# A head's tail interleaved with the next head's first projection, the halves of its output normed apart, and 12 products ahead of the decay gates

## The reference

```
proj = einsum('btd,dn->btn', xn, w_in)          # 1024 -> q, k, v, z_gla, a_lo, gate_logits, ...
g = log_sigmoid(a_lo @ w_a2 + b_a) / GATE_NORM  # decay gates, per head 128 keys
b = cumsum(g) in a chunk
o = (q k^T * decay) v + (q * exp(b)) S          # S: state, 128 x 256 per head
S_new = exp(b_last) * S + (k * exp(b_last - b))^T v
o = o * rsqrt(mean(o * o) + EPS) * gla_norm_g   # per head, over its 256 value channels
y_b = (o * silu(z_gla)) @ w_gla_o
```

## Time and profile before

| | |
|---|---|
| median of 3 runs | 1179.35 us (1177.84 to 1181.88) |
| the profiled execution: device time | 1183.72 us |
| the profiled execution: span | 1182.0 us, mean granted TensorE clock 0.986 |
| PE busy | 1148.5 us (97%) |
| DVE, ACT, POOL busy | 542.8, 425.2, 199.9 us |
| one head on PE, from one diagonal step to the next | 106.8 to 108.3 us |

### The profile page before, as it was taken

One profiled execution on the slowest core, in us unless ns is written; L12 is line 12 of the kernel. 1 busy time (PEld: TensorE's weight loads), 2 busy tenths in 40 slices (PEclk: granted clock), 3 DMA queues, 4 the chain that ended last, 5 costly groups with the idle time before them and its releaser, 6 DMA issues.

```text
span 1182.0 us, 17776 instructions
## 1 busy us (share of the span) xinstructions
PE 1148.5 (97%) x6872; PEld 1108.8 (94%) x6872; DVE 542.8 (46%) x716; ACT 425.2 (36%) x561; POOL 199.9 (17%) x128
## 2 busy tenths in 40 slices
PE   5899999999999999999999999999999999999997
PEld 5899999999999999999999999999999999999886
DVE  5777777775000001663494358437635001444433
ACT  5555555554111112542543453345426111211321
POOL 3511111111212120211112011111101211210000
PEclk8999999999999999999999899999989999999999
DMA  6211111111211222210311131021102103342231
GB/s 211 65 40 47 50 40 40 40 36 37 83 63 54 72 73 62 72 37 18 113 35 35 36 95 35 18 87 48 31 18 76 49 22 110 109 161 83 98 106 71
DMA packets 95631, 76.16 MB, mean 64 GB/s; under 512 B 3944, under 2 KB 88808, under 8 KB 95608
## 3 DMA queue, kind: packets, MB, share of 16 engines
q1 hardware_dynamic: 84588, 61.59, 17.5%
q10 hardware_dynamic: 11020, 14.26, 3.6%
HBM read 62.04 MB, written 13.80 MB: 64 GB/s over the span
## 4 chain that ended last, share of the span: by engine, by line
PE 87%; issue 6%; DVE 4%; ACT 2%; DMA 0%; DVEq 0%; ACTq 0%
PE ps L464 25%; PE ps L465 25%; PE ps L466 25%; PE ps L599 2%; PE ps L662 1%; PE ps L641 1%; PE ps L633 1%; PE ps L643 1%; PE ps L626 1%; DVE xcs L1232 1%; PE ps L681 1%; ACT xcs L891 1%; PE ps L570 1%; DVE xc L1224 1%; PE ps L491 1%
## 5 line engine op out<-in xcount | busy, mean ns | idle before, releaser
L464 PE MATMUL ps<-xn,whi 128*128 128x364 f32 x1344 | 452.2, 336 | 2.4 <-DVE xn L1159 1.5
L465 PE MATMUL ps<-xn,whi 128*128 128x364 f32 x1344 | 443.5, 330 | 0.0
L466 PE MATMUL ps<-xn,wlo 128*128 128x364 f32 x1344 | 443.1, 330 | 0.0
L432 POOL TENSOR_TENSOR wlo<-raw,whi 128x1024 fp32r<-128x1024 f32 x72 | 181.3, 2518 | 862.8 <-ACT whi L838 862.8
L464 PEld LDWEIGHTS ps<-xn,whi 128*128 128x128 f32 x1344 | 254.1, 189 | 6.8 <-issue 2.2
L465 PEld LDWEIGHTS ps<-xn,whi 128*128 128x128 f32 x1344 | 254.3, 189 | 0.2
L466 PEld LDWEIGHTS ps<-xn,wlo 128*128 128x128 f32 x1344 | 254.0, 189 | 0.0
L838 ACT ACTIVATE whi<-raw 128x1024 fp32r<-128x1024 f32 x72 | 76.0, 1055 | 152.1 <-PE ps L466 86.4
L465 PE MATMUL ps<-act_s,whi 128*128 128x364 f32 x384 | 126.2, 329 | 0.0
L464 PE MATMUL ps<-act_s,whi 128*128 128x364 f32 x384 | 126.2, 329 | 0.0
L466 PE MATMUL ps<-act_s,wlo 128*128 128x364 f32 x384 | 126.1, 328 | 0.0
(11 more groups left out here) (246 smaller groups left out, 1389.5 us busy)
## 6 DMA issues: line engine op xcount, KB each, us to landing
raw<-in_w_in SPq DMA_DIRECT2D x56, 512.0 KB, 3.8
branch_a<-keep ACTq DMA_DIRECT2D x8, 546.0 KB, 2.8
mal<-branch_a SPq DMA_DIRECT2D x8, 544.0 KB, 4.5
xt<-in_x_prompt SPq DMA_DIRECT2D x8, 512.0 KB, 6.8
raw<-in_w_lru_o SPq DMA_DIRECT2D x8, 512.0 KB, 3.7
st<-in_state_gla ACTq DMA_DIRECT2D x4, 1024.0 KB, 5.6
out<-st ACTq DMA_DIRECT2D x4, 1024.0 KB, 4.7
raw<-in_w_gla_o SPq DMA_DIRECT2D x8, 512.0 KB, 5.7
```

Of the source, the lines that this page charges most:

```text
L432: pool.tensor_tensor(wlo[:, c % 2], raw[:, c % 2], whi[:, c % 2].bitcast(F32), ALU.subtract).then_inc(s["lo_ok"], 1)
L464: pe.matmul(dst, wh, mh, start=first, stop=False)
L465: pe.matmul(dst, wh, ml, start=False, stop=False)
L466: return pe.matmul(dst, wl, mh, start=False, stop=last)
```

## The change

PE: job 0 of head 0 runs ahead of the loop. In the loop job 5 ends ahead of the outputs, and the tail is interleaved with job 0 of the next head (`part(6, bankA, ...)`; after the last head that is merge-gate job 0): seven groups of three products in Os, then mean squares, then the sample state sums, with products between all. The next head starts with 12 products of job 1, then g0 and g1, 12 more, g2. Steps are renumbered so that nrm0 to nrm2 come ahead of sKV0 to sKV3; g0 and g1 now wait for DVE's sKV2 and sKV3.

ACT: the loads of `wa2_raw` go to SP, the rounding of `wa2` into the tail of the head before. Tanh of job 5 moves ahead of the outputs. Rounding the weights of job 2 moves from ahead of the gates to behind Ln; that of job 3, and the load of the sample states, behind the second level. Ln and Exp write into a half of `qk`, not `kt`. The last head is written out behind a loop of three.

DVE: the two halves are normed and gated apart (`gated_output`): half 0 after sKV1, half 1 after sKV3, each with its own semaphore.

```
@@ sync
                     load(6 * h + (N_GLA + j), (N_GLA + j) % 2, ...)
+                    if j == 0:
+                        sp.wait_ge(s["wa2_lo"], h + ONE)
+                        for r in range(6):
+                            sp.dma_start(wa2_raw[...], t["w_a2"][0][:, bass.ds(h * P, P)]).then_inc(s["wa2_in"], 16)
@@ tensor, Os
-                    between = iter(range(2, KT - 1))
+                    between = iter(range(KT))
-                            if q in (2, 5) or (q == NSEQ - 1 and d == 0):
+                            if q % 2 == 1 and (d == 0 or q < NSEQ - 1):
                                 k = next(between)
-                                part(5, bankB, 2, range(k, k + 1))
+                                part(6, bankA, 0, range(k, k + 1))
@@ tensor, start of a head
-                start_job(0)
+                pe.wait_ge(s["wa2_lo"], h + (ONE + 1))
+                start_job(1)
                 pe.wait_ge(s["zg_silu"], 2 * h + ONE)
-                part(0, bankA, 0)
-                part(0, bankA, 1)
-                part(0, bankA, 2)
+                part(1, bankB, 0, EARLY)
                 gate(0)
                 gate(1)
-                start_job(1)
-                part(1, bankB, 0)
+                part(1, bankB, 0, LATE)
                 gate(2)
@@ tensor, tail
-                part(5, bankB, 2, range(2))
+                part(5, bankB, 2)
...
+                start_job(6)
                 c_step("Os", sample_output)
+                part(6, bankA, 0, range(KT - 1, KT))
+                pe.wait_ge(s["sq_sum"], 2 * h + 1)
+                mean_square(0)
+                part(6, bankA, 1, range(0, 2))
+                mean_square(1)
+                part(6, bankA, 1, range(2, 6))
+                pe.wait_ge(s["sq_sum"], 2 * (h + 1))
+                mean_square(2)
+                part(6, bankA, 1, range(6, KT))
                 sample_outer(0)
+                part(6, bankA, 2, range(0, 1))
                 sample_outer(1)
-                part(5, bankB, 2, range(KT - 1, KT))
+                part(6, bankA, 2, range(1, 3))
                 sample_outer(2)
+                part(6, bankA, 2, range(3, 5))
                 sample_outer(3)
-                for j in range(PIECES):
-                    mean_square(j)
+                part(6, bankA, 2, range(5, KT))
 
-            with pe.Fori(0, KT // 2) as i:
+            job(0, N_GB + 1, bankB, xn)
+            with pe.Fori(1, KT // 2) as i:
@@ scalar
-                hi(3 * h, N_GLA + 2)
-                act.wait_ge(s["st0_out"], 16 * h + ONE)
-                act.dma_start(st0[:, :, :], ...)
-                act.wait_ge(s["og_ok"], 2 * h + ONE)
+                act.wait_ge(s["og0_ok"], h + ONE)
...
                 act.activation(dd[:, :], dd[:, :], ACT.Ln, bias=1.0).then_inc(s["g_ln"], 1)
+                hi(3 * h, N_GLA + 2)
                 job_at(1)
+                act.wait_ge(s["og1_ok"], h + ONE)
                 act.activation(p3(kb[:, :]), slot3(bankB), ACT.Copy).then_inc(s["k_ok"], 1)
-                hi(3 * h, N_GLA + 3)
                 level_exp(0)
                 level_exp(1)
+                hi(3 * h, N_GLA + 3)
...
-            act.wait_ge(s["og_ok"], 2 * HEADS + ONE)
+            act.wait_ge(s["og0_ok"], HEADS + ONE)
+            act.wait_ge(s["og1_ok"], HEADS + ONE)
             act.wait_ge(s["st_out"], 16 * HEADS + ONE)
             act.wait_ge(s["st0_out"], 16 * HEADS + ONE)
@@ vector, tail
+                def gated_output(d):
+                    dve.scalar_tensor_tensor(oo[d], oo[d], vec[...], inv, ALU.mult, ALU.mult).then_inc(s["o_norm"], 1)
+                    dve.wait_ge(s["o_norm"], 2 * h + (d + 1))
+                    dve.tensor_tensor(keep[:, 2 * h + d, :], keep[:, 2 * h + d, :], oo[d], ALU.mult).then_inc(s[f"og{d}_ok"], 1)
+                add_outer(0)
+                add_outer(1)
+                if not last:
+                    wa2_low(h + 1)
+                gated_output(0)
+                add_outer(2)
+                add_outer(3)
+                gated_output(1)
```

More of the change, by code:

```diff
@@ L82 @@
 STARTS_AT_ONE = ("wa2_lo", "ma_ok", "wo_lo", "r_tanh", "i_tanh", "ga_tanh", "zg_silu", "x_tail", "i_done", "z_silu", "hz_ok",
-                 "st0_out", "st_out", "og_ok", "merged0", "merged1", "gb_tanh0", "gb_tanh1", "c_full", "c_act", "c_dve")
+                 "st0_out", "st_out", "og0_ok", "og1_ok", "merged0", "merged1", "gb_tanh0", "gb_tanh1", "c_full", "c_act", "c_dve")
 NTAIL = 1 + NSEQ + HIST + NSEQ * HIST
@@ L100, in head_steps @@
     steps += [(f"O{g}{d}", "act") for g in range(2) for d in range(VH)] + [("Os", "act")]
+    steps += [(f"nrm{j}", "act") for j in range(PIECES)]
     steps += [(f"sKV{n}", "dve") for n in range(NSEQ // 2)]
-    steps += [(f"nrm{j}", "act") for j in range(PIECES)]
     return steps
@@ L215, in build @@
         oo = [gb, kb]
+        inv = qk[:, 1, :]
         ring = [dd, kt]
@@ L385, in _ @@
                     load(6 * h + (N_GLA + j), (N_GLA + j) % 2, w_in[:, :, bass.ds(h * step + col, P)])
+                    if j == 0:
+                        sp.wait_ge(s["wa2_lo"], h + ONE)
+                        sp.sem_inc(s["sp_passed"], 1)
+                        for r in range(6):
+                            sp.dma_start(wa2_raw[r * RANK:(r + 1) * RANK, :], t["w_a2"][0][:, bass.ds(h * P, P)]).then_inc(s["wa2_in"], 16)
             with sp.Fori(0, KT // 2) as i:
@@ L574, in _ @@
             pe.wait_ge(s["alo_ok"], 2)
+            pe.wait_ge(s["lo_ok"], N_GLA + 1)
+            piece(N_GLA, bankA, xn, 0)
+            piece(N_GLA, bankA, xn, 1)
+            pe.wait_ge(s["alo_ok"], PIECES)
+            piece(N_GLA, bankA, xn, 2).then_inc(s["job_done"], 1)
+            pe.wait_ge(s["tails_ok"], 2)
+            pe.wait_ge(s["ma_ok"], KT + ONE)
             with pe.Fori(0, HEADS) as h:
@@ L950, in _, with wa2_high, act_head @@
                 act.dma_start(dst, trow[r0:r0 + nr, :]).then_inc(s["tails_out"], 16)
-            with act.Fori(0, HEADS) as h:
+            def wa2_high(h):
+                act.wait_ge(s["wa2_in"], 96 * h + 96)
+                act.activation(wa2[:, :], wa2_raw[:, :], ACT.Copy).then_inc(s["wa2_hi"], 1)
+            def act_head(h, last):
                 def job_at(c):
@@ L980, in level_exp @@
                     ins.then_inc(s["lev_e"], 1)
[L982 to L986, removed]
                 job_at(0)
                 act.activation(p3(qb[:, :]), slot3(bankA), ACT.Copy, scale=float(DK) ** -0.5).then_inc(s["q_ok"], 1)
-                hi(3 * h, N_GLA + 2)
-                act.wait_ge(s["st0_out"], 16 * h + ONE)
-                act.dma_start(st0[:, :, :], t["state_gla"][0].rearrange("b h p v -> h p b v")[h]).then_inc(s["st0_in"], 16)
-                act.wait_ge(s["og_ok"], 2 * h + ONE)
+                act.wait_ge(s["og0_ok"], h + ONE)
                 for j in range(PIECES):
@@ L1004, in _ @@
                 act.activation(dd[:, :], dd[:, :], ACT.Ln, bias=1.0).then_inc(s["g_ln"], 1)
+                hi(3 * h, N_GLA + 2)
                 job_at(1)
+                act.wait_ge(s["og1_ok"], h + ONE)
                 act.activation(p3(kb[:, :]), slot3(bankB), ACT.Copy).then_inc(s["k_ok"], 1)
-                hi(3 * h, N_GLA + 3)
                 level_exp(0)
                 level_exp(1)
+                hi(3 * h, N_GLA + 3)
+                act.wait_ge(s["st0_out"], 16 * h + ONE)
+                act.dma_start(st0[:, :, :], t["state_gla"][0].rearrange("b h p v -> h p b v")[h]).then_inc(s["st0_in"], 16)
                 level_exp(2)
@@ L1049, in _ @@
                 ins.then_inc(s["smp_hi"], 1)
+                job_at(5)
+                act.wait_ge(s["zg_silu"], 2 * h + (ONE + 1))
+                act.activation(p3(vT[:, :]), slot3(bankB), ACT.Tanh, scale=0.5).then_inc(s["zg_tanh"], 1)
                 for g in range(2):
@@ L1060, in _ @@
                 squares(slice(0, SEQ))
+                hi(3 * h, N_GLA + 7)
                 full("Os")
@@ L1065, in _ @@
                 squares(slice(SEQ, TOK))
-                job_at(5)
-                act.wait_ge(s["zg_silu"], 2 * h + (ONE + 1))
-                act.activation(p3(vT[:, :]), slot3(bankB), ACT.Tanh, scale=0.5).then_inc(s["zg_tanh"], 1)
+                if not last:
+                    wa2_high(h + 1)
+                act.wait_ge(s["sq_sum"], 2 * h + 2)
                 for j in range(PIECES):
                     full(f"nrm{j}")
-                    act.activation(kt[:, j * PIECE:(j + 1) * PIECE], ps[:, bank(f"nrm{j}"), 0:PIECE], ACT.Ln,
+                    act.activation(inv[:, j * PIECE:(j + 1) * PIECE], ps[:, bank(f"nrm{j}"), 0:PIECE], ACT.Ln,
                                    bias=ssum[:, 31:32]).then_inc(s["c_act"], 1)
-                hi(3 * h, N_GLA + 7)
                 act.wait_ge(*emptied(h, "nrm2"))
-                act.activation(kt[:, :], kt[:, :], ACT.Exp, scale=-0.5).then_inc(s["n_rstd"], 1)
+                act.activation(inv[:, :], inv[:, :], ACT.Exp, scale=-0.5).then_inc(s["n_rstd"], 1)
```

(43 more changed lines are left out.)

11 lines of the change are left out of this document (2 added, 9 removed).

## The result

The changed kernel takes 1183.26 us (median of 12 runs, 1182.66 to 1184.19), the kernel before 1178.65 us in the same rounds (12 runs, 1176.28 to 1182.71). The ratio is 1.0037, 95% interval 1.0024 to 1.0049: slower by 4.6 us. Forecast were +4.2 us and 1183.5.

A forecast was written before the change was run, and what follows sets the result against it. TensorE was taken as the bound, busy 1148.5 of 1182 us. Terms -3.7 - 8.6 + 2.6 + 5.7 + 6.6 + 1.6 gave +4.2 us: 1183.5 as a median, own range 1181 to 1187, overall 1176 to 1191.

The forecast's parts named there:

- the end of the last head: Behind the last mean square: PE stands 6.6 us before the third merge-gate job, bounds 5.8 and 8.
- the half clock behind it: Products after the idle stretch at the last head's end: half clock for some 3.4 us, +1.6 us, between 0 and 3.2.
- gates: At the next head's start: g0 waits for DVE's sKV2, cost 0, margin 1.4 us.
- job 2's weights: Rounded behind Ln, they make PE stand 1.4 us ahead of job 2 in every head, +5.7 us.
- I carry the difference over to the median: Terms made against the profiled execution, 1183.72 us, 4.37 above the median of 1179.35, were applied to the median.
- clock: In the four tails: clock stays up, removing six half-clock stretches at 1.43 us each, -8.6 us, bounds 0 and -8.6.
- mean squares: At each head's end: products between cover 0.92 us of waits for DVE and ACT, -3.7 us over four heads.
- switching: In each tail: eight more product groups behind small matmuls cost 0.08 us each, +2.6 us, bounds 0 and +4.
- the clock's fall: Rival: the clock still falls once a tail, four stretches stay, +9.9 us, 1189.3; chance 0.22.
- POOL went ahead of the scan: Rival claimed the reverse: DVE's scan first, job 2 waits 2.4 us more a head, +13.9, 1193.2; chance 0.07.
- job 2's weights were late: Rival claimed the reverse: job 2's weights are not late, -1.5 us in all, 1177.9; chance 0.14.
- the end was not covered: Rival claimed the reverse: last head's end is covered, PE does not stop, -4.0 in all, 1175.3; chance 0.10.

The follow-up runs named there:

- the run with seven groups in Os: The kernel before with seven groups of three products in Os, none ahead of the outputs: 1177.50 us, 0.9980 of before.
- the last run: The changed kernel with both waits out, plus six products of job 5 moved ahead of the first transpose of the attention matrix: 1166.35 us, 0.9888 of before.
- the kernel with both repairs: The changed kernel with job 2's weights rounded ahead of the gates, copies not waiting for state transfers, and Tanh after two copies: 1170.04 us, 0.9912 of before.

## Why the prediction came out as it did

Right in mechanism and size: *the end of the last head* (6.6 us forecast, 6.80 in the row, the copies started by the transfer), the half clock behind it (1.6 forecast; nine products from 911.30 to 914.19 took 2.9 us where 1.5 would do, so 1.4; wait and clock together 8.2 forecast, 8.6 measured by taking both out), the *gates* (cost 0; taking the 12 products away makes the wait), and PE's wait at *job 2's weights* (1.4 a head forecast, 1.3 by the rows, 4.4 to 4.6 us in all by taking it out, not 5.7: a little comes back as a wait of a gate).

Wrong in one step: "I carry the difference over to the median". The *clock* term, -8.6, was made against an execution with six stretches at half clock, and these six are the very reason why it lay 4.37 us above the median. They measure at most 7.3 us (1183.7 against 1176.4 us at clocks 0.986 and 0.998), and against the median only about 3. The term was some 5.6 us too large for the number that was predicted. Of that, 1.3 us or more is the price of a stretch, 1.2 measured, not 1.43. The two heads whose difference gave 1.43 differ in another thing too: ahead of the mean squares PE waits 0.49 us in the first and 0.23 in the second:

```profile
778.94 2.56 PE L681 MATMUL ps<-qk,ones 128*128 128x364 f32 x6 [0.23 <-DVE st L1440]
```

That difference of 0.26 us is a matter of the *mean squares*, and it came into the price of the clock.

Wrong in size: *switching*, +2.6. The 0.24 us behind the first product was read behind 8-column matmuls and applied to all eight groups. Behind the 256-column state sums it is 0.16, and with the sums side by side three switches a head are saved and the kernel is 3.0 us slower. Of the two more groups in Os no cost shows either: the heads with five groups were as long. What I left out is the other half of it: state sums that stand side by side wait for DVE to take in the one before. The kernel before had one group of three products, between its second and third sum, so it did not lose the whole 3.0 us. In its order of the sums, at full clock (the run with seven groups in Os), the waits that are left look like this:

```profile
668.05 0.28 PE L675 MATMUL ps<-svlo,skeys 128*128 128x256 f32 x1
668.38 0.39 PE L674 MATMUL ps<-svhi,skeys 128*128 128x256 f32 x1
```

The starts are 0.33 us apart where 0.12 is usual. Over the four sums of that head it makes 0.6 us, an estimate of 2.6 us in four heads.

How the terms stand by measurement, against runs of the kernel before at full clock (1176.4): all the interleaving, mean squares and state sums together, 1170.0 - 1176.4 = -6.4. With 2.6 of it for the state sums, 3.8 is left, which fits the 3.7 of the mean squares; neither part was measured by itself on the kernel before. Job 2's weights are +4.6, the end +8.7 with its clock. That is +6.9, and 1183.3 us; it must come out so, since the last two are the steps from 1170.0 back to the change, and is no check of the parts. The median of before holds some 3 us of half clock that the change takes away: +4. The misses cancelled. The clock gave 5.6 us too much gain. Against it, switching had 2.6 us too much loss, the state sums' gain of 2.6 was left out, and job 2's weights were 1.1 too dear, less 0.5 for the end, which cost more than forecast: 5.8. The total was better than its parts.

Of the rivals, the clock's fall did not occur with seven groups (it does with five), POOL went ahead of the scan, job 2's weights were late, and the end was not covered.

Open: why a whole tail falls in one execution and not in another. The runs show only that it depends on the groups of products in Os, and that with seven groups neither kernel fell in a profiled tail. The 1.4 us beyond expectation in the last run was not taken apart by a run. The rows of the kernel with both repairs explain most of it:

```profile
534.52 0.71 PE L639 MATMUL ps<-ident,kt 128*128 128x128 f32 x5
535.80 0.44 PE L620 MATMUL ps<-ident,att 128*128 128x128 f32 x2 [0.58 <-ACT kT L989]
```

From 534.96, where the transposes of kT end by their spacing, to 535.80 they give 0.84 us a head, not 0.58; four times that is 3.4 of the 3.7 us.

## What to carry to other kernels

When a term comes from something that varies between executions, such as stretches at half clock, see how many of them the profiled one holds before its gain is promised to the median: the distance of the profiled time to the median is a hint of it. Moving the next job into a tail takes cover from what runs behind the tail: list the chains that the moved job used to hide, at the turn of the loop and above all behind its last pass, where ACT's chain of copies was hidden with 1 us to spare. And a move can pay with its side effects repaired: the change lost 0.4%, with the two waits taken out it gains 0.9%.

## What the runs showed of the hardware

With the mean squares side by side, the load of ACT's tables comes ahead of the wait for its input in the loop and behind it in straight code (565.51 and 885.34 above; the other two heads of the loop are as the first), 1.28 us that are hidden in one and not in the other. Why is not shown. The idle time in a row of PE understates what a wait costs, because the row ahead of it is longer than what its matmul costs: 1.12 us in brackets against 1.3 between starts, 0.58 against 0.84. A product costs 0.24 us instead of 0.17 behind 8-column matmuls, and 0.16 behind a 256-column one. And the same kernel on the same chip differs by 7 us along with its mean granted clock (0.986 to 0.998), without any change of its work.
